# A transformer block and a second model's two layers on one core: weight buffers of three pairs interleaved by column, moving columns of a fifth pair in alternating runs

## The reference

```python
hl = modulate(rms_norm(xl, norm1_g), mod[0], mod[1])
zl = hl @ w_in + b_in                              # 2048 -> 13312 channels
y_na = neighbourhood_attention(q, k, v, kc, vc, na_rpb)
# gated sum of a convolution, a spatial gating unit and the attention
xl = xl + mod[2] * ((g_conv * y_conv + g_sgu * y_sgu + g_att * y_att) @ w_o + b_o)
hl2 = modulate(rms_norm(xl, norm2_g), mod[3], mod[4])
xl = xl + mod[5] * (square(relu(hl2 @ w_ff1 + b_ff1)) @ w_ff2 + b_ff2)   # 2048 -> 8192 -> 2048
x = rms_norm(xl, final_g)
```

```python
h = h + rms_norm_2(diff_attention_mixer(rms_norm_2(h, g0), w_ain, w_aout, ...), p0)
h = h + rms_norm_2(pool_mixer(rms_norm_2(h, g1), w_pin, w_grp, scale, w_pout), p1)
return h[:, 16:]
```

## Time and profile before

| | |
|---|---|
| time, median of 2 runs | 2738.11 us (2733.66 to 2742.55) |
| the profiled execution: its time, its span | 2743.35 us, 2741.5 us |
| mean granted TensorE clock | 0.992 |
| PE, PEld, DVE, ACT, POOL busy | 98%, 94%, 70%, 46%, 6% |
| matmuls, ACT roundings, DVE subtractions | 21464, 856, 856 |

### The profile page before, as it was taken

One profiled execution on the slowest core, in us unless ns is written; L12 is line 12 of the kernel. 1 busy time (PEld: TensorE's weight loads), 2 busy tenths in 40 slices (PEclk: granted clock), 3 DMA queues, 4 the chain that ended last, 5 costly groups with the idle time before them and its releaser, 6 DMA issues.

```text
span 2741.5 us, 51493 instructions
## 1 busy us (share of the span) xinstructions
PE 2687.8 (98%) x21464; PEld 2567.7 (94%) x21464; DVE 1906.2 (70%) x2933; ACT 1268.6 (46%) x1836; POOL 154.7 (6%) x162
## 2 busy tenths in 40 slices
PE   7999999999999999999999999999999999999998
PEld 4599977899999999999999999999999999989997
DVE  6765689889897778886554655677656665478564
ACT  5522344455446444544443444464444444544453
POOL 0000011200014001100000000030000000100001
PEclk9999999999999999999999999999999999999999
DMA  8766765466666788787556555564444444536564
GB/s 307 287 219 218 240 190 177 135 201 186 198 185 195 253 281 266 260 284 230 185 185 197 180 192 186 186 198 154 157 136 146 157 148 150 173 120 189 186 196 130
DMA packets 163990, 539.01 MB, mean 197 GB/s; under 512 B 31024, under 2 KB 35120, under 8 KB 163632
## 3 DMA queue, kind: packets, MB, share of 16 engines
q1 hardware_dynamic: 163760, 535.73, 59.8%
HBM read 533.57 MB, written 2.10 MB: 195 GB/s over the span
## 4 chain that ended last, share of the span: by engine, by line
PE 91%; DVE 5%; DMA 1%; issue 1%; ACT 1%; SPq 0%; POOL 0%; DVEq 0%; ACTq 0%
PE ps L566 27%; PE ps L571 27%; PE ps L568 27%; DVE lo L1690 1%; PE ps L782 1%; PE ps L801 1%; PE ps L729 1%; DMA raw<-in_w_mod 1%; PE ps L717 1%; PE ps L790 1%; DVE row L2265 1%; PE ps L957 0%; PE ps L745 0%; DMA raw<-in_w_in 0%; PE ps L979 0%
## 5 line engine op out<-in xcount | busy, mean ns | idle before, releaser
L1076 ACT ACTIVATE hi<-raw 128x1024 fp32r<-128x1024 f32 x856 | 900.9, 1057 | 914.1 <-PE ps L571 471.1
L566 PE MATMUL ps<-AH,hi 128*128 128x256 f32 (+2 forms) x4432 | 1263.2, 285 | 1.8 <-DVE AL L2104 1.8
L571 PE MATMUL ps<-AH,lo 128*128 128x256 f32 (+2 forms) x4432 | 1251.8, 282 | 7.5 <-DVE lo L1690 7.4
L568 PE MATMUL ps<-AL,hi 128*128 128x256 f32 (+2 forms) x4432 | 1252.9, 283 | 0.0
L1690 DVE TENSOR_TENSOR lo<-raw,hi 128x1024 fp32r<-128x1024 f32 x856 | 1038.8, 1227 | 201.8 <-ACT hi L1076 200.1
L566 PEld LDWEIGHTS ps<-AH,hi 128*128 128x128 f32 x4432 | 836.7, 189 | 31.1 <-issue 28.3
L571 PEld LDWEIGHTS ps<-AH,lo 128*128 128x128 f32 x4432 | 837.1, 189 | 10.8 <-DVE lo L1690 10.7
L568 PEld LDWEIGHTS ps<-AL,hi 128*128 128x128 f32 x4432 | 836.4, 189 | 0.9
L566 PE MATMUL ps<-YH,hi 128*128 128x256 f32 (+1 forms) x1512 | 422.6, 279 | 0.0
L568 PE MATMUL ps<-YL,hi 128*128 128x256 f32 (+1 forms) x1512 | 422.6, 279 | 0.0
L571 PE MATMUL ps<-YH,lo 128*128 128x256 f32 (+1 forms) x1512 | 422.4, 279 | 0.1
(11 more groups left out here) (276 smaller groups left out, 2510.0 us busy)
## 6 DMA issues: line engine op xcount, KB each, us to landing
raw<-in_w_ff SPq DMA_DIRECT2D x256, 512.0 KB, 4.3
raw<-in_w_in SPq DMA_DIRECT2D x208, 512.0 KB, 4.2
raw<-in_w_mod SPq DMA_DIRECT2D x192, 512.0 KB, 4.9
raw<-in_w_ain SPq DMA_DIRECT2D x128, 512.0 KB, 3.7
raw<-in_w_pin SPq DMA_DIRECT2D x64, 512.0 KB, 3.5
raw<-in_w_o SPq DMA_DIRECT2D x32, 512.0 KB, 4.7
raw<-in_w_aout SPq DMA_DIRECT2D x32, 512.0 KB, 3.6
raw<-in_w_pout SPq DMA_DIRECT2D x32, 512.0 KB, 3.5
```

What stands on the lines that cost most here:

```text
L566: e.matmul(b.ap[:, o], hi[:, k, :], xh, start=start and k + i == 0, stop=False, skip_group_check=many)
L568: e.matmul(b.ap[:, o], hi[:, k, :], xl, start=False, stop=False, skip_group_check=many)
L571: mm = e.matmul(b.ap[:, o], los[j % NSPLIT][:, k, :], xh, start=False, stop=stop and k == KU - 1, skip_group_check=many)
L1076: e.activation(his[u % NSPLIT][:, :, :], raws[raw_at[i]][:, :].rearrange("p (k m) -> p k m", k=KU), ACT.Copy).then_inc(s_hi, 1)
```

## The change

In the units from number 52 up, the pair's layout depends on the pair. `GROUPS` gives the number of tiles that share a block: in pairs 0 and 4 one tile (as before), in pair 1 two, in pair 2 four, in pair 3 eight. Within a block of g tiles, column m of tile b lies at `m * g + b`, so that neighbouring columns of a tile are g fp32 elements apart: 8, 16 or 32 bytes in pairs 1, 2 and 3. ACT and DVE read the raw values in their old order and write `hi` and `lo` into these places; DVE also reads `hi` from them. The matmuls take each tile with its step. Which value is multiplied with which is unchanged.

In pair 4 the weights lie as before. Where 256 columns are moved, moving and output columns are both walked in another order: 0 to 15, 128 to 143, 16 to 31, 144 to 159, and so on. Products with 258 or 272 columns, the joint units and the grouped weights keep their order.

```diff
--- before.py
+++ after.py
@@ -32,6 +32,23 @@
 
 MODS = (8, 9, 10, 11, 16, 17, 18, 19, 12, 13, 14, 15, 20, 21, 22, 23)
 FIRST = 64 - 8 * len(WHOLE) + NLEAD
+GROUPS = (1, 2, 4, 8, 1)
+TURNED = (False, False, False, False, True)
+
+
+def spread(t, u, k=None):
+    g = GROUPS[u % NSPLIT] if u >= FIRST else 1
+    w = t[:, :, :].rearrange("p k m -> p (k m)").rearrange("p (a m b) -> p a b m", b=g, m=128)
+    return w if k is None else w[:, k // g, k % g, :]
+
+
+def inorder(t, u):
+    g = GROUPS[u % NSPLIT] if u >= FIRST else 1
+    return t[:, :].rearrange("p (a b m) -> p a b m", b=g, m=128)
+
+
+def banks(x, turned):
+    return x.rearrange("p (h l c) -> p l h c", h=2, c=16) if turned else x
 NEXTRA = 5
 EPS = 1e-6
 SCALE2 = 128.0 ** -0.5
@@ -563,12 +580,14 @@
                         ready(k0 + k)
                     many = len(parts(0)) > 1
                     for i, (xh, xl, o) in enumerate(parts(k0 + k)):
-                        e.matmul(b.ap[:, o], hi[:, k, :], xh, start=start and k + i == 0, stop=False,
+                        turned = xh.shape[1] == T and TURNED[j % NSPLIT]
+                        y, xh, xl = banks(b.ap[:, o], turned), banks(xh, turned), banks(xl, turned)
+                        e.matmul(y, spread(hi, j, k), xh, start=start and k + i == 0, stop=False,
                                  skip_group_check=many)
-                        e.matmul(b.ap[:, o], hi[:, k, :], xl, start=False, stop=False, skip_group_check=many)
+                        e.matmul(y, spread(hi, j, k), xl, start=False, stop=False, skip_group_check=many)
                         if k + i == 0:
                             e.wait_ge(s_lo, j + 1)
-                        mm = e.matmul(b.ap[:, o], los[j % NSPLIT][:, k, :], xh, start=False,
+                        mm = e.matmul(y, spread(lo, j, k), xh, start=False,
                                       stop=stop and k == KU - 1, skip_group_check=many)
                 mm.then_inc(s_unit, 1)
                 tick()
@@ -594,11 +613,11 @@
                         hi, lo = his[(j0 + i) % NSPLIT], los[(j0 + i) % NSPLIT]
                         if k == 0:
                             e.wait_ge(s_hi, j0 + i + 1)
-                        e.matmul(b.ap[:, o], hi[:, k, :], xh, start=start and k == 0, stop=False)
-                        e.matmul(b.ap[:, o], hi[:, k, :], xl, start=False, stop=False)
+                        e.matmul(b.ap[:, o], spread(hi, j0 + i, k), xh, start=start and k == 0, stop=False)
+                        e.matmul(b.ap[:, o], spread(hi, j0 + i, k), xl, start=False, stop=False)
                         if k == 0:
                             e.wait_ge(s_lo, j0 + i + 1)
-                        mm = e.matmul(b.ap[:, o], lo[:, k, :], xh, start=False, stop=stop and k == KU - 1)
+                        mm = e.matmul(b.ap[:, o], spread(lo, j0 + i, k), xh, start=False, stop=stop and k == KU - 1)
                         if k == KU - 1:
                             mm.then_inc(s_unit, 1)
                 for _ in bs:
@@ -1045,11 +1064,11 @@
                             kt = 4 * g + k
                             if mp == mi == 0:
                                 e.wait_ge(s_al, 48 + kt + 1)
-                            e.matmul(b.ap[:, 0:T], hi[:, 4 * mi + k, :], Y1H[:, kt, :], start=(k == 0), stop=False)
-                            e.matmul(b.ap[:, 0:T], hi[:, 4 * mi + k, :], Y1L[:, kt, :], start=False, stop=False)
+                            e.matmul(b.ap[:, 0:T], spread(hi, j, 4 * mi + k), Y1H[:, kt, :], start=(k == 0), stop=False)
+                            e.matmul(b.ap[:, 0:T], spread(hi, j, 4 * mi + k), Y1L[:, kt, :], start=False, stop=False)
                             if mi == k == 0:
                                 e.wait_ge(s_lo, j + 1)
-                            mm = e.matmul(b.ap[:, 0:T], lo[:, 4 * mi + k, :], Y1H[:, kt, :], start=False, stop=(k == 3))
+                            mm = e.matmul(b.ap[:, 0:T], spread(lo, j, 4 * mi + k), Y1H[:, kt, :], start=False, stop=(k == 3))
                         mm.then_inc(s_unit if mi else s_grp, 1)
                         b.free = (s_gx, 4 * g + 2 * mp + mi + 1)
                     tick()
@@ -1073,8 +1092,7 @@
                 e.wait_ge(*landed(i))
                 if u >= NSPLIT:
                     e.wait_ge(s_unit, u - NSPLIT + 1)
-                e.activation(his[u % NSPLIT][:, :, :], raws[raw_at[i]][:, :].rearrange("p (k m) -> p k m", k=KU),
-                             ACT.Copy).then_inc(s_hi, 1)
+                e.activation(spread(his[u % NSPLIT], u), inorder(raws[raw_at[i]], u), ACT.Copy).then_inc(s_hi, 1)
 
             def first_parts(j):
 
@@ -1687,8 +1705,8 @@
             def second_part(i):
                 u = number_at[i]
                 e.wait_ge(s_hi, u + 1)
-                e.tensor_tensor(los[u % NSPLIT][:, :, :], raws[raw_at[i]][:, :].rearrange("p (k m) -> p k m", k=KU),
-                                his[u % NSPLIT][:, :, :].bitcast(F32), ALU.subtract).then_inc(s_lo, 1)
+                e.tensor_tensor(spread(los[u % NSPLIT], u), inorder(raws[raw_at[i]], u),
+                                spread(his[u % NSPLIT], u).bitcast(F32), ALU.subtract).then_inc(s_lo, 1)
 
             def second_parts(j):
```

## The result

The changed kernel takes 3715.61 us (median of 2 runs, 3714.34 to 3716.87) against 2738.11: 977.5 us more, 1.357 times as long, 95% interval 1.3473 to 1.3667. The forecast of 3540 had the sign, the place and four fifths of the size (803 of 977 us); 3716 lies above its range (2725 to 3640).

The account below looks back on a forecast made before the run. TensorE was taken as the bound, its weight loads (111.4 ns) without slack against matmul spacing. 2738 + 803 us for spaced loads in pairs 2 and 3, other terms nothing, gave 3540 us; range 2725 to 3640, own range 3380 to 3640.

Parts of the forecast that it names:

- Step 1: Weight loads from spaced columns: 8016 matmuls in pairs 2 and 3 at 219 instead of 117 ns, +803 us net.
- The match of 1.67 with twice 0.83 ns: Spaced DVE read's 1.67 ns an element equals two 0.83 ns weight-load steps; taken as the memory-line fetch time.
- Only 32 bytes cost: Rival on weight loads: four elements apart still go free, pair 3 alone pays, +401 us, 3140 us; chance 0.10.
- Loads don't care: Rival on weight loads: a column every 0.83 ns whatever the spacing; 2738 to 2770 us, likeliest 2745; chance 0.33.
- Step 2: ACT rounding and DVE subtraction into spaced columns: 3 to 30 us if TensorE stays, nothing beside slow loads.
- Step 3: Fifth pair's moving and output columns in runs of 16: taken at nothing, bounds -9 to +250 us.
- Step 4: Pair 1's weight loads, 8 bytes apart: taken at nothing; +405 us at the price of pairs 2 and 3.
- The clock falls: Rival on TensorE: chip grants 1.2 GHz, time passes 4000 us; chance 0.05, shared with pair 1 or fifth pair dear.
- a gain: Rival: faster by over 2%, with only the fifth pair's -9 us seen as a source; chance 0.05.
- DVE the bound: Rival: loads free, but both spaced streams of DVE's subtraction charged, plus jitter; 2795 to 2830 us; chance 0.05.

Follow-up runs that it names:

- reads alone: Changed kernel with only the matmuls' weight reads spaced; ACT and DVE write in plain order, fifth pair plain: 3700.58 us, 955 us above the kernel before.
- the load alone: Kernel before, with only the turn of the modulation sums reading weights 1, 2, 3 or 4 elements apart beside one moving column: 2746.43 us.

## Why the forecast was right in kind and short in size

*What bounds the kernel.* Right. The weight path had no slack: loads in 111.4 ns against a spacing of 113.0, and the price of a spaced load showed in full (233 alone, 235 in the stream).

*Step 1, the load's price: the step that failed.* The mechanism is shown: reads alone give 955 us, and the load alone costs the same. The term was mis-sized. I took 1.67 ns a column from the one spaced DVE row and got 219 ns; loads take 233 at 16 bytes, which is (233 - 5) / 128 = 1.78 ns a column, and products stand 240 ns apart at 32. Over all widths, from each product's start to the next matmul's in the profiled executions, pair 2 went from 120.5 to 236.9 ns and pair 3 from 120.8 to 243.0. For some 4008 matmuls each that is 467 + 490 = 957 us; the forecast had 818. The match of 1.67 with twice 0.83 ns, on which I leaned, was a coincidence or a bound that isn't reached; the runs don't say which.

The 15 us that I let the slower PE save on stalls were hardly there either: PE's idle time is 51 us after, 54 before.

*Only 32 bytes cost.* Out: 16 bytes cost nearly as much. Of the Trainium skill, SBUF — State Buffer, the note on cachelines in the section on the DMA port swizzle, the first sentence (full bandwidth with two hits on a 16-byte line, a penalty for each new line) agrees with the runs: two columns on a 16-byte line cost 118 instead of 112 ns alone, one column a line 233. Its other figure, that a step of 4 fp32 elements is free, does not: the measured 233 ns decide.

*Loads don't care.* Out too. In the Trainium skill, TensorE: Matmul & The Clock Gate, section on LDWEIGHTS, a load's time is its columns over 1.2 GHz, by which 128 columns come to an estimated 107 ns. The section sets columns against the contraction dimension and doesn't speak of spacing. The runs come near the figure for neighbouring columns (112 ns) and are far from it from a step of three on (175 ns).

*Step 2, ACT and DVE.* The price a piece was within the bounds for DVE, +0.84 to +1.04 us (0.62 to 1.25 forecast), and above them for ACT, +1.0 to +1.2 (0.86 forecast). Beside slow loads it was hidden, as said. Without that cover it costs 66 us, not 3 to 30: I summed the windows in which DVE's busy time passes PE's. DVE did come to 49 of 50 us in four stretches, but of PE's 106 us of idle time only 4 lie in them; that a lead of three units is too short for the slower chain of ACT and DVE is my reading, and was not tested.

*Step 3, the fifth pair.* Taken at nothing; 8.3 us measured, 4.4 ns a product. The row of DVE's 64-byte runs said nothing of TensorE's moving side.

*Step 4, pair 1.* Taken at nothing. Alone it leaves the time as it was, though its 256-column products are 6 ns slower: 118 ns is the load's own pace, and the pair sits at 120.8. In the changed kernel it is 11 us.

*The clock falls, a gain, DVE the bound.* None happened; the clock was 0.992, as before.

*The sum again with measured terms:* 467 + 490 + 11 (pair 1, 2.8 ns over all widths) + 10 (pair 4, 2.4 ns) - 2 (pair 0) = 976 us, for the 971 by which the span grew. The range failed since I bounded the load's price above by the same single row from which I took its value, and put its upper end only 100 us over the forecast, without a term that gives these; a bound needs a second row or a margin.

## What to carry to other kernels

Where a load of fresh weights goes with every matmul, compare the pace of loads with that of matmuls before touching the layout of weights: here 111 against 113 ns, so that the price of the widely spaced loads went straight into the time. Keep at least two fp32 weight columns on one 16-byte line (118 ns a load); one column a line doubles the load (233 ns). A layout price is best found by reading only, or writing only, in the new layout: the two runs split 955 us from 66 in one go, and per-pair variants in one kernel give five prices from one trace.

## What the hardware showed that I had not expected

A weight load is paid by the line: 112, 118, 175 and 233 ns alone for columns 4, 8, 12 and 16 bytes apart, then 227, 227, 235 and 240 in the stream for 20, 24, 28 and 32. ACT and DVE pay much the same a piece. Plain, ACT's rounding is 0.83 ns an element, from 1024 elements in 1057 ns and 256 in 418 ns (YH<-tmp, L1441 of the kernel before). DVE's subtraction is (1218 - 148) / 1024 = 1.04 ns an element. With the medians of the changed kernel, elements 16 bytes apart then come to 1.84 and 1.86 ns ((2092 - 1062) / 1024 + 0.83 and (2061 - 1218) / 1024 + 1.04), 32 bytes apart to 2.0 and 2.05. For DVE it hardly matters whether it is one stream or two (at 32 bytes 2117 or 2137 ns against 2254).

Most 256-column products have one of two paces, 113 to 114 or 118 ns, with any pair and at the same granted clock (1.00): in the kernel before 425 matmuls in the 50 us from 845 us on, 117.6 ns each, but 113.0 from 1415 to 1500 us.

```profile
845.00:895.00 50.00, 50.00 (x425) 49.94 (x424) 38.43 (x48) 32.66 (x50) 17.20 (x13) 1.00 0.63 196
```

By the medians of the units, 294 of them stand at the first pace and 162 at the second; 32 more, all between 2526 and 2617 us, at 120 ns. Of the 16 changes of pace between two such units in a row, 13 come where another kind of product lies between two units. The run with the load alone, whose product pairs are plain, has nearly the same counts (298 and 158, and the same 32); with other layouts they differ (pair 0: 114.1 to 117.2 ns). Over the 12288 products of 256 columns, 3 ns are 37 us, an estimate. What chooses the pace is open.
